# Two token halves as two runs of matmuls in w_out's and the feed-forward's units of a hybrid encoder step

## The chip, the cores and the metric

The kernel runs on one core of one Trainium2 chip. The metric is the device time of one execution in microseconds (us). TensorE multiplies, VectorE (DVE), ScalarE (ACT) and GpSimd (POOL) do the elementwise work, and SyncE (SP) issues the loads and stores.

## The reference

The program computes two layers of an encoder for 512 prompt tokens and 64 sample tokens. All of it is in f32.

```python
xn = rmsnorm(xp, norm_mix[l])
q, k, v, qi, ki, wi, u, gv = project(xn, w_in[l], pos_p)
a = dsa_prompt(q, qi, wi, k, v, ki, pos_p)
gvn = rmsnorm(jax.nn.gelu(gv), gate_norm[l])
bmix = jax.nn.gelu(u) * spatial_prompt(gvn, w_spatial[l], b_spatial[l])
xp = xp + jnp.concatenate([a, bmix], axis=-1) @ w_out[l]
xp = xp + sq_relu_ffn(rmsnorm(xp, norm_ffn[l]), w_ff1[l], w_ff2[l])

def sq_relu_ffn(x, w1, w2):
    h = jax.nn.relu(x @ w1)
    return (h * h) @ w2
```

The sample tokens go through the same lines with a cache of 128 positions. D_MODEL is 1024, D_FF is 4096. The change concerns the last two lines of a layer: the product with `w_out` and the two products of the feed-forward.

## The kernel before, in words

All 576 tokens (`TOK`) are kept side by side in the free dimension, with the model dimension on the partitions: `x`, `xh`, `xl`, `vh` and `vl` are 128 x 8 x 576, and the index of the 8 blocks of 128 (`KT`) is called k. A product in f32 precision is made of three matmuls on f32r numbers. Each f32 operand is split into a high part (`xh`, `vh`, `ring_hi`) and a low part (`xl`, `vl`, `ring_lo`), and the sum takes high by high, high weight by low activation, and low weight by high activation.

The weights stream from memory through a ring. SP loads 512 KB into `ring_raw`, ACT makes `ring_hi` from it (`split_hi`, line 521), DVE or POOL makes `ring_lo` (`split_lo`, line 766). There are four ring slots, and a slot is free when the unit that reads it is done (`unit_done`).

After the projection and the attention stage of a layer come 72 units (line 1309): 8 units of `w_out` (u = 0 to 7), then four groups of 8 units of `w_ff1` and 8 units of `w_ff2`. A unit makes 128 output features for all tokens. The 576 tokens are two halves of 288 (`HALVES`), because a PSUM bank holds 512 numbers, and unit u writes the banks 2 (u mod 4) and 2 (u mod 4) + 1. Per unit there are 8 k, three products and two halves: 48 matmuls of 128 x 288, and each carries its own weight load. Only the unit's last matmul raises `unit_done`, so nobody reads a bank ahead of the unit's end. In two layers this makes 144 units and 6912 matmuls.

TensorE's program is written out in order, with waits (`pe.wait_ge`) between the instructions. In the units these waits bear on the change:

- u = 0 (the first unit of `w_out`): its k run 4, 5, 6, 7, 0, 1, 2, 3, and ahead of k = 0 it waits for the last piece of `vl` (line 1325), which DVE makes in `mt_low` (line 928).
- u = 8, written `u == KT` (the first unit of `w_ff1`): ahead of each k it waits for `xl` of this k (line 1328). `xl` of block j is made by DVE in `feed` (line 772) from `x` and `xh` of block j, after ACT has made `xh` (line 536) and after DVE has added unit j's result to `x` (line 994). In DVE's program the order is: add unit j, `feed` of j - 1, `split_lo` of the next weights; and `feed` of block 7 stands behind the last `split_lo`.
- the first `w_ff2` unit of each group (`f == KT`): ahead of each k it waits for `vl` of this k (line 1331), which DVE makes at line 1017 from the results of the group's `w_ff1` unit k, after ACT's relu (line 730) and square (line 735).

Every other wait of a unit (`slot`, `unit_read`, line 1319) stands at its start.

Of the kernel before, what the change touches and what calls it, by code (L numbers as in the profile page):

```python
# [17 lines left out]
def hybrid_encoder_program(nc, A, O):  # L18
# [7 lines left out]
    SEQ, D = A["x_prompt"].shape[1], A["x_prompt"].shape[2]  # L26
    DEC = A["x_sample"].shape[1]
    DEPTH, _, PAST, NKV, HD = A["cache_k"].shape
    ID = A["cache_kidx"].shape[3]
    N_IN = A["w_in"].shape[2]  # L30
# [7 lines left out]
    KT = D // P  # L38
    FT = DFF // P
# [5 lines left out]
    NT = NPT + 1  # L45
# [45 lines left out]
    with ctx:  # L91
# [3 lines left out]
        def sem(name):  # L95
            return ctx.enter_context(nc.semaphore(name))
# [110 lines left out]
        xh_ready, vh_ready, vl_ready = sem("xh_ready"), sem("vh_ready"), sem("vl_ready")  # L207
# [12 lines left out]
        xl_ready = sem("xl_ready")  # L220
# [56 lines left out]
        def unit_read(u):  # L277

            l, u = u // UNITS, u % UNITS
            if u >= KT and (u - KT) % (2 * KT) < KT:  # L280
                f = (u - KT) // (2 * KT) * KT + (u - KT) % (2 * KT)
                return f1_relu, FT * l + f + 1
            j = u if u < KT else (u - KT) // (2 * KT) * KT + u % KT + KT
            return y_read, KT * (GROUPS + 1) * l + j + 1
# [776 lines left out]
        def _(pe):  # L1061
# [28 lines left out]
            for l in range(DEPTH):  # L1090
                def slot(n):

                    pe.wait_ge(lo_ready, SLOTS * l + n + 1)
                    return tuple(b[:, n % NSLOT, :] for b in (ring_hi, ring_lo))
# [60 lines left out]
                for n in range(S_OUT):  # L1155
                    w = slot(n)
# [152 lines left out]
                for u in range(UNITS):  # L1309
                    wh, wl = (b.rearrange("p (k n) -> p k n", k=KT) for b in slot(S_OUT + u))  # L1310
                    g, f = divmod(u - KT, 2 * KT)
                    first_product = u >= KT and f < KT
                    ah, al = (xh, xl) if first_product else (vh, vl)
                    if u >= 4:

                        pe.wait_ge(*unit_read(UNITS * l + u - 4))
                    if u == KT + 3:

                        pe.wait_ge(ssb_read, l + 1)

                    order = list(range(KT)) if u >= KT else list(range(KT // 2, KT)) + list(range(KT // 2))
                    for k in order:
                        if u == 0 and k == 0:

                            pe.wait_ge(vl_ready, (2 * NT + FT) * l + 2 * NT)
                        if u == KT:

                            pe.wait_ge(xl_ready, KT * (2 * l + 1) + k + 1)
                        if u >= KT and f == KT:

                            pe.wait_ge(vl_ready, (2 * NT + FT) * l + 2 * NT + KT * g + k + 1)
                        for w, a in ((wh, ah), (wh, al), (wl, ah)):
                            for half in range(2):
                                last = mm(bank[2 * (u % 4) + half][:, 0:HALF], w[:, k, :], a[:, k, HALVES[half]],  # L1334
                                          start=k == order[0] and w is wh and a is ah, stop=k == order[-1] and w is wl)
                    last.then_inc(unit_done, 1)
                    if u == KT + 1:

                        pe.wait_ge(ss_added, KT * (2 * l + 2))
                        for half in range(2):  # L1340
                            last = mm(bank[6 + half][:, 0:HALF], ones[:, :], ssacc[:, HALVES[half]], start=True, stop=True)
                        last.then_inc(ssb_done, 1)
# [53 lines left out]
```

## Time and profile before

| | |
|---|---|
| timed runs | 1470.62, 1472.02, 1513.19 us; median 1472.02 |
| the profiled execution: first to last instruction (span) | 1508.3 us, mean granted TensorE clock 0.919 |
| the profiled execution: time with what lies around the span | not given by itself; the slowest timed run, 1513.19 us, is 4.9 us above this span |
| TensorE matmul busy | 98% of the span, 9329 matmuls |
| TensorE weight load busy | 88%, 9329 loads |
| VectorE, ScalarE, GpSimd busy | 44%, 35%, 12% |

PE is TensorE's matmul row and PEld its weight-load row, which overlap. The end of a matmul is modelled, so the distance between the starts of two matmuls is what tells its real price. "PEclk" is the granted TensorE clock, as a share of 2.4 GHz: 1.0 is 2.4 GHz and 0.5 is 1.2 GHz. Times in the rows count from the first instruction.

### The profile page before, as it was taken

What the parts mean: (1) busy time and instruction counts of PE and PEld (TensorE: products, weight loads), DVE (VectorE), ACT (ScalarE), POOL (GpSimd) and SP (SyncE); (2) the same over time, 40 slices, a digit from 0 to 9 for tenths busy, and PEclk for the clock granted to TensorE, in tenths of its full rate; (3) what the DMA queues carried; (4) which work ended last, traced back from release to release, by engine and by line L of the source; (5) the groups of instructions that cost most, each with busy time, mean ns of one, the idle gap of its engine ahead of it and who ended that gap; (6) DMA issues with size and microseconds to landing.
All of it is one profiled execution on the core that took longest, in us unless ns stands there. A gap on an engine that the chain in (4) does not pass through costs nothing.

```text
span 1508.3 us, 22280 instructions
## 1 busy us (share of the span) xinstructions
PE 1483.1 (98%) x9329; PEld 1323.6 (88%) x9329; DVE 664.4 (44%) x1172; ACT 521.8 (35%) x956; POOL 185.1 (12%) x215
## 2 busy tenths in 40 slices
PE   6999999999999999999999999999999999999997
PEld 5766766899999999999976677669999999999997
DVE  5257632245444444444623683213454444344453
ACT  5365542233213223133335553323332231321322
POOL 4246200020000000000214540000100000000011
PEclk8999755799999999999999995559999999999998
DMA  6211200033232222222321120001322222222221
GB/s 180 70 57 43 74 5 0 0 85 85 85 84 78 82 80 85 84 84 83 104 82 45 40 78 25 5 1 42 85 75 82 83 84 84 85 85 85 82 59 63
DMA packets 169252, 102.37 MB, mean 68 GB/s; under 512 B 6920, under 2 KB 159424, under 8 KB 169152
## 3 DMA queue, kind: packets, MB, share of 16 engines
q1 hardware_dynamic: 169152, 100.94, 23.0%
q8 instruction: 74, 1.21, 0.3%
q14 instruction: 26, 0.21, 0.0%
HBM read 96.98 MB, written 3.95 MB: 67 GB/s over the span
## 4 chain that ended last, share of the span: by engine, by line
PE 97%; DVE 1%; DMA 1%; ACT 1%; issue 0%; SPq 0%; DVEq 0%; ACTq 0%
PE bank L1334 61%; PE bank L1108 15%; PE bank L1219 6%; PE bank L1255 4%; PE bank L1235 3%; PE bank L1126 2%; PE bank L1270 2%; PE bank L1286 1%; PE bank L1140 1%; DMA late<-in_x_prompt 1%; PE bank L1200 1%; PE bank L1353 0%; PE bank L1069 0%; PE bank L1085 0%; ACT L677 0%
## 5 line engine op out<-in xcount | busy, mean ns | idle before, releaser
L521 ACT ACTIVATE ring_hi<-ring_raw 128x1024 fp32r<-128x1024 f32 x176 | 184.8, 1050 | 305.4 <-PE bank L1334 248.6
L1334 PE MATMUL bank<-vh,ring_hi 128*128 128x288 f32 x1280 | 275.4, 296 | 0.0
L1334 PE MATMUL bank<-vl,ring_hi 128*128 128x288 f32 x1280 | 275.2, 296 | 0.0
L1334 PE MATMUL bank<-vh,ring_lo 128*128 128x288 f32 x1280 | 275.2, 296 | 0.0
L766 DVE TENSOR_TENSOR ring_lo<-ring_raw,ring_hi 128x1024 fp32r<-128x1024 f32 x164 | 213.6, 1302 | 132.5 <-ACT ring_hi L521 125.5
L1334 PE MATMUL bank<-xh,ring_hi 128*128 128x288 f32 x1024 | 220.8, 297 | 0.0
L1334 PE MATMUL bank<-xl,ring_hi 128*128 128x288 f32 x1024 | 220.2, 296 | 0.0
L1334 PE MATMUL bank<-xh,ring_lo 128*128 128x288 f32 x1024 | 220.2, 296 | 0.0
L1334 PEld LDWEIGHTS bank<-vh,ring_hi 128*128 128x128 f32 x1280 | 205.2, 189 | 0.0
L1334 PEld LDWEIGHTS bank<-vh,ring_lo 128*128 128x128 f32 x1280 | 205.2, 188 | 0.0
L1334 PEld LDWEIGHTS bank<-vl,ring_hi 128*128 128x128 f32 x1280 | 205.2, 189 | 0.0
L1334 PEld LDWEIGHTS bank<-xh,ring_hi 128*128 128x128 f32 x1024 | 164.3, 188 | 0.7 <-DVE xl L772 0.5
L1334 PEld LDWEIGHTS bank<-xh,ring_lo 128*128 128x128 f32 x1024 | 164.2, 188 | 0.0
L1334 PEld LDWEIGHTS bank<-xl,ring_hi 128*128 128x128 f32 x1024 | 164.2, 189 | 0.0
L1013 DVE TENSOR_TENSOR late<-late 128x576 f32<-128x576 f32 x64 | 48.6, 760 | 219.8 <-ACT late L730 219.8
L1025 DVE TENSOR_TENSOR late<-late,bank 128x288 f32<-128x288 f32 x128 | 52.4, 451 | 200.9 <-PE bank L1334 200.9
L730 ACT ACTIVATE late<-bank 128x288 f32<-128x288 f32 x128 | 45.7, 409 | 265.8 <-PE bank L1334 265.8
L1108 PE MATMUL bank<-ring_hi,xh 128*128 128x512 f32 (+1 forms) x320 | 133.7, 418 | 3.0 <-DVE xl L772 3.0
L1108 PE MATMUL bank<-ring_hi,xl 128*128 128x512 f32 (+1 forms) x320 | 126.9, 396 | 0.0
L1108 PE MATMUL bank<-ring_lo,xh 128*128 128x512 f32 (+1 forms) x320 | 126.8, 396 | 0.0
L406 POOL COPY ssacc<-late 128x576 f32<-128x576 f32 x5 | 3.5, 696 | 789.9 <-ACT late L540 789.9
L1219 PE MATMUL bank<-late 64*128 64x128 f32 (+4 forms) x160 | 100.2, 726 | 0.0
(161 smaller groups left out, 1608.9 us busy)
## 6 DMA issues: line engine op xcount, KB each, us to landing
ring_raw<-in_w_ff SPq DMA_DIRECT2D x128, 512.0 KB, 4.1
ring_raw<-in_w_in SPq DMA_DIRECT2D x32, 512.0 KB, 3.7
ring_raw<-in_w_out SPq DMA_DIRECT2D x16, 512.0 KB, 4.2
late<-in_x_prompt SPq DMA_DIRECT2D x4, 512.0 KB, 5.7
out_y_prompt<-late SPq DMA_DIRECT2D x4, 512.0 KB, 2.9
w_sp<-in_w_spatial SPq DMA_DIRECT2D x2, 512.0 KB, 4.2
gate_bc<-in_gate_norm SPq DMA_DIRECT2D x2, 256.0 KB, 4.9
out_k_prompt<-z SPq DMA_DIRECT2D x2, 256.0 KB, 4.3
```

The source lines that it names most:

```text
L521: s.activation(ring_hi[:, n % NSLOT, :], ring_raw[:, n % NRAW, :], ACT.Copy).then_inc(hi_ready, 1)
L730: last = s.activation(rl2[:, f % 2, HALVES[half]], bank[2 * (u % 4) + half][:, 0:HALF], ACT.Relu)
L766: v.tensor_tensor(ring_lo[:, n % NSLOT, :], ring_raw[:, n % NRAW, :], ring_hi[:, n % NSLOT, :].bitcast(F32), ALU.subtract).then_inc(lo_rea ...
L1013: link(v.tensor_tensor(h32[:, f % 2, :], rl2[:, f % 2, :], rl2[:, f % 2, :], ALU.mult))
L1025: last = v.tensor_tensor(yb[:, j % 2, HALVES[half]], r2b[:, HALVES[half]], bank[b + half][:, 0:HALF], ALU.mult)
L1108: last = mm(bank[t][0:ROWS[t], :], a[:, kx, cols(t)], b[:, kk, :], start=kx == 0 and b is wh and a is xh, stop=kx == KT - 1 and a is xl)
L1126: last = mm(bank[5 + i % 2][0:rows, 0:KEYS[t]], a[b:b + ID, hh // 4, cols(t)], k[b:b + ID, 0:KEYS[t]], start=a is qih and k is kh, stop=a ...
L1219: mm(bank[i % 2][0:ROWS[t], 0:KEYS[t]], qT[b:b + HD, hh % 4, cols(t)], keys[b:b + HD, 0:KEYS[t]], start=True, stop=True).then_inc(qk_done, 1)
L1235: last = tp(bank[2 + i % 2][0:n, c0:c0 + ROWS[t]], pr[0:ROWS[t], i % 2, s0:s0 + n], ident[0:ROWS[t], 0:ROWS[t]])
L1255: last = mm(bank[4 + a % 2][0:ROWS[t], hh * HD:(hh + 1) * HD], pT[0:n, i % 2, s * ROWS[t]:(s + 1) * ROWS[t]], vals, start=s == 0, stop=s = ...
L1270: last = mm(bank[6][0:rows, g * CPG:(g + 1) * CPG], w_spT[0:rows, g, 0:rows], gvn[0:rows, t, g * CPG:(g + 1) * CPG], start=True, stop=True)
L1334: last = mm(bank[2 * (u % 4) + half][:, 0:HALF], w[:, k, :], a[:, k, HALVES[half]], start=k == order[0] and w is wh and a is ah, stop=k == ...
```

## The change

The loop over the two halves moves from the innermost place of a unit to the outermost. Before, each weight tile was used for half 0 and then for half 1; now all 24 matmuls of half 0 (8 k by three products) come first, then all 24 of half 1. The waits inside the loop stay ahead of the first matmul of their k, which is now the one of half 0; half 1 waits for nothing. Lines behind the change are one higher than before (1335 for 1334).

```diff
-                    for k in order:
-                        if u == 0 and k == 0:
-
-                            pe.wait_ge(vl_ready, (2 * NT + FT) * l + 2 * NT)
-                        if u == KT:
-
-                            pe.wait_ge(xl_ready, KT * (2 * l + 1) + k + 1)
-                        if u >= KT and f == KT:
-
-                            pe.wait_ge(vl_ready, (2 * NT + FT) * l + 2 * NT + KT * g + k + 1)
-                        for w, a in ((wh, ah), (wh, al), (wl, ah)):
-                            for half in range(2):
+                    for half in range(2):
+                        for k in order:
+                            if half == 0:
+                                if u == 0 and k == 0:
+
+                                    pe.wait_ge(vl_ready, (2 * NT + FT) * l + 2 * NT)
+                                if u == KT:
+
+                                    pe.wait_ge(xl_ready, KT * (2 * l + 1) + k + 1)
+                                if u >= KT and f == KT:
+
+                                    pe.wait_ge(vl_ready, (2 * NT + FT) * l + 2 * NT + KT * g + k + 1)
+                            for w, a in ((wh, ah), (wh, al), (wl, ah)):
                                 last = mm(bank[2 * (u % 4) + half][:, 0:HALF], w[:, k, :], a[:, k, HALVES[half]],
                                           start=k == order[0] and w is wh and a is ah, stop=k == order[-1] and w is wl)
                     last.then_inc(unit_done, 1)
```

First place, on TensorE: the end of the first `w_ff1` unit (u = 8) of layer 0. In the kernel before, its last wait for `xl` (of k = 7) stands ahead of the 43rd of 48 matmuls, and the rows below are the last two matmuls of k = 6 and the six of k = 7:

```order
L1334 MATMUL bank0<-xh,ring_lo 128x288
L1334 MATMUL bank1<-xh,ring_lo 128x288
L1334 MATMUL bank0<-xh,ring_hi 128x288 [waits xl_ready]
L1334 MATMUL bank1<-xh,ring_hi 128x288
L1334 MATMUL bank0<-xl,ring_hi 128x288
L1334 MATMUL bank1<-xl,ring_hi 128x288
L1334 MATMUL bank0<-xh,ring_lo 128x288
L1334 MATMUL bank1<-xh,ring_lo 128x288
```

In the changed kernel the same wait stands ahead of the 22nd matmul, and half 1 (bank 1) begins behind it:

```order
L1335 MATMUL bank0<-xh,ring_lo 128x288
L1335 MATMUL bank0<-xh,ring_hi 128x288 [waits xl_ready]
L1335 MATMUL bank0<-xl,ring_hi 128x288
L1335 MATMUL bank0<-xh,ring_lo 128x288
L1335 MATMUL bank1<-xh,ring_hi 128x288
L1335 MATMUL bank1<-xl,ring_hi 128x288
L1335 MATMUL bank1<-xh,ring_lo 128x288
```

The wait has moved from 42 matmuls into the unit to 21; the number of matmuls and what each of them reads is the same.

Second place, on TensorE: the first `w_ff2` unit of the first group (u = 16), around its last wait for `vl` (k = 7). Before:

```order
L1334 MATMUL bank0<-vh,ring_lo 128x288
L1334 MATMUL bank1<-vh,ring_lo 128x288
L1334 MATMUL bank0<-vh,ring_hi 128x288 [waits vl_ready]
L1334 MATMUL bank1<-vh,ring_hi 128x288
L1334 MATMUL bank0<-vl,ring_hi 128x288
```

In the changed kernel:

```order
L1335 MATMUL bank0<-vh,ring_lo 128x288
L1335 MATMUL bank0<-vh,ring_hi 128x288 [waits vl_ready]
L1335 MATMUL bank0<-vl,ring_hi 128x288
L1335 MATMUL bank0<-vh,ring_lo 128x288
L1335 MATMUL bank1<-vh,ring_hi 128x288
```

Here too the last wait comes after 21 matmuls in place of 42. In the first unit of `w_out` the wait for the last `vl` comes after 12 matmuls in place of 24. On the other engines no instruction of the stage moves.

## Rows read from the trace of the kernel before

**Rows 1.** Page, parts 1 and 2: busy time by engine; granted clock in 40 slices.
```profile
PE 1483.1 (98%) x9329; PEld 1323.6 (88%) x9329; DVE 664.4 (44%) x1172; ACT 521.8 (35%) x956; POOL 185.1 (12%) x215
...
PEclk8999755799999999999999995559999999999998
```

**Rows 2.** Page, part 4: the chain that ended last, shares of the span by engine.
```profile
PE 97%; DVE 1%; DMA 1%; ACT 1%; issue 0%; SPq 0%; DVEq 0%; ACTq 0%
```

**Rows 3.** That chain in order of time: start us, us, what.
```profile
50.49 4.21 PE bank L1200 x32
...
356.39 396.81 PE bank L1334 x2976
```

**Rows 4.** w_ff1's first unit, layer 0: start us, us, line, count [idle before <-releaser].
```profile
342.04 0.32 PEld L1334 LDWEIGHTS bank<-xh,ring_hi 128*128 128x128 f32 x2
...
344.71 0.32 PEld L1334 LDWEIGHTS bank<-xl,ring_hi 128*128 128x128 f32 x2
...
347.95 0.30 PEld L1334 LDWEIGHTS bank<-xh,ring_hi 128*128 128x128 f32 x2 [0.25 <-DVE xl L772]
```

**Rows 5.** DVE in the same stretch.
```profile
342.37 0.82 DVE L994 TENSOR_TENSOR x<-x,bank 128x288 f32<-128x288 f32 x2 [1.60 <-PE bank L1334]
343.11 0.81 DVE L772 SCALAR_TENSOR_TENSOR xl<-x,gcol,xh 128x576 fp32r<-128x576 f32 x1
345.56 1.61 DVE L766 TENSOR_TENSOR ring_lo<-ring_raw,ring_hi 128x1024 fp32r<-128x1024 f32 x1 [1.64 <-ACT ring_hi L521]
347.09 0.80 DVE L772 SCALAR_TENSOR_TENSOR xl<-x,gcol,xh 128x576 fp32r<-128x576 f32 x1
```

**Rows 6.** Weight loads of the same unit in layer 1.
```profile
1079.49 0.32 PEld L1334 LDWEIGHTS bank<-xh,ring_hi 128*128 128x128 f32 x2
...
1085.39 0.30 PEld L1334 LDWEIGHTS bank<-xh,ring_hi 128*128 128x128 f32 x2 [0.25 <-DVE xl L772]
```

**Rows 7.** Weight loads of the first unit of w_ff2, layer 0, first group.
```profile
394.50 0.32 PEld L1334 LDWEIGHTS bank<-vh,ring_hi 128*128 128x128 f32 x2
...
397.17 0.32 PEld L1334 LDWEIGHTS bank<-vl,ring_hi 128*128 128x128 f32 x2
```

**Rows 8.** DVE in that stretch: the vl of k = 7.
```profile
396.37 0.76 DVE L1017 TENSOR_TENSOR vl<-late,vh 128x576 fp32r<-128x576 f32 x1
```

**Rows 9.** Weight loads at the start of w_out's first unit, layer 0.
```profile
290.47 0.42 PEld L1286 LDWEIGHTS bank<-ident,att 128*128 128x128 f32 x4 [1.61 <-DVE vl L928]
...
292.44 0.32 PEld L1334 LDWEIGHTS bank<-vh,ring_hi 128*128 128x128 f32 x2
```

**Rows 10.** DVE there: the last piece of vl.
```profile
291.80 0.69 DVE L928 TENSOR_TENSOR vl<-bank,vh 128x512 fp32r<-128x512 f32 x1 [1.44 <-ACT vh L702]
```

**Rows 11.** Page, part 5: one of six groups of the units' weight loads.
```profile
L1334 PEld LDWEIGHTS bank<-vh,ring_hi 128*128 128x128 f32 x1280 | 205.2, 189 | 0.0
```

**Rows 12.** Matmuls of the projection's start, in time; six in a row share a bank.
```profile
19.52 0.77 PE L1108 MATMUL bank<-ring_hi,xh 128*128 128x512 f32 x1 [3.02 <-DVE xl L772]
20.09 0.63 PE L1108 MATMUL bank<-ring_lo,xh 128*128 128x512 f32 x1
...
22.22 0.62 PE L1108 MATMUL bank<-ring_hi,xh 128*128 128x512 f32 x1
...
23.37 0.40 PE L1108 MATMUL bank<-ring_lo,xh 128*128 128x512 f32 x1
23.61 0.40 PE L1108 MATMUL bank<-ring_hi,xl 128*128 128x512 f32 x1
23.84 0.40 PE L1108 MATMUL bank<-ring_hi,xh 128*128 128x512 f32 x1
```

**Rows 13.** Three stretches: busy us by engine, then granted clock, DMA share, GB/s.
```profile
19.50:22.70 3.20, 3.18 (x8) 2.52 (x9) 2.11 (x2) 3.20 (x6) 1.98 (x3) 0.50 0.00 0
...
289.00:292.50 3.50, 2.00 (x17) 2.03 (x17) 2.02 (x4) 0.60 (x1) 0.00 (x0) 1.00 0.02 5
1494.00:1500.50 6.50, 5.65 (x27) 5.66 (x28) 1.90 (x4) 1.86 (x4) 1.28 (x5) 0.50 0.01 3
```

## The prediction, made before the changed kernel was run

> **What bounds the kernel now.** I read the busy shares first: PE is busy for 98% of the span and no other engine for half of it [rows 1]. A busy PE may still be a waiting one, so next comes the chain of waits: PE holds 97% of it [rows 2]. In order of time the units of w_out and of the feed-forward are one unbroken run: 2976 matmuls in 396.81 us, which is 133.3 ns from one start to the next [rows 3]. So a unit of 48 matmuls lasts 6.40 us, half a unit 3.20 us, and the 6912 matmuls 922 us, more than half of the time. The granted clock is full there; it is low in the attention stage and at the ends [rows 1]. Whatever changes the 133.3 ns, or makes PE wait in the units, changes the time by the same amount. Whatever makes another engine faster or slower does not, as long as its result arrives before PE asks for it.
>
> The reader should also see that PE already waits in one place: in the first unit of w_ff1 the weight load for k = 7 stands with an idle time put down to DVE's xl, in layer 0 at 347.95 and in layer 1 at 1085.39 [rows 4, 6]. A wait that is already late in the old order is what the new order moves ahead.
>
> **The change part by part.** It removes and adds no matmul, no weight load, no semaphore and no DMA. It moves two things: which matmul follows which, and how early in a unit the waits for xl and vl stand. The unit still reports its end with its last matmul, so DVE and ACT get nothing sooner.
>
> *The distance of two matmuls.* Before, neighbours write alternate banks; now 24 in a row accumulate into one bank. The units of before don't show this, but two other places do. In the projection six matmuls in a row share a bank, with the same pattern of operands (a stationary tile used twice, then a new one): the starts 23.37 and 23.61 lie inside such a run, and 23.61 to 23.84 crosses to the next bank; both distances are 0.23 to 0.24 us [rows 12]. At line 1200 the small projection runs 16 matmuls of 288 columns into one bank and then 16 into another: 4.21 us for 32, 131.6 ns each [rows 3]. Its stationary tiles are narrower (80 and 40 columns), which may account for the 1.7 ns to 133.3. The bounds are therefore -1.7 ns by line 1200, and above, by the projection: its 512 columns take 0.232 us at full clock, and (22.22 - 20.09)/5 = 0.426 us at clock 0.5 [rows 12, 13], so streaming alone would be 0.213 us at full clock, and 19 ns come on top. For 288 columns streaming is 0.120 us, and 13 ns come on top now. If the difference of 6 ns were the price of staying in a bank, it would be +6 ns. I take 0, the value of the bank crossing, which tests just this: 6912 x 0 = 0, with ends of -12 and +41 us.
>
> *The first unit of w_ff1 (u = 8), once a layer.* Its first weight load starts at 342.04 [rows 4]. In the new order k = 7 comes after 21 matmuls, at 342.04 + 21 x 0.1333 = 344.84; in the old one after 42, at 347.64, where it really came at 347.95. What sets the 347.95 is DVE's second xl, which runs from 347.09 for 0.80 us and ends at 347.89 [rows 5], so PE resumes 0.06 us behind it. Does this xl come sooner in the new kernel? DVE's program has it behind a split of the weights (345.56 for 1.61 us), which itself waits for ACT's half of that split, and the chain starts with the addition at 342.37, when unit 7 is done [rows 5]. None of these looks at unit 8, so they stay where they are. PE then waits from 344.84 until 347.95: 3.11 us, where the old wait cost 0.31. The difference is 2.80 us, which is just the 21 matmuls that the old order still had to do ahead of it. k = 6 needs the first xl, which ends at 343.92 and is asked for at 344.44: no wait. Layer 1 is the same: 1079.49 + 2.80 = 1082.29 against 1085.39 now, 3.10 us of waiting, and 1085.39 less 1085.09 before [rows 6]. Sum: 2 x 2.80 = +5.6 us. Nothing gives it back later: behind the wait stand only PE's own matmuls, all other engines wait for PE, and the tail of the kernel comes after them.
>
> *The first unit of w_ff2 in each group, eight times.* k = 7 is now asked for at 394.50 + 21 x 0.1333 = 397.30, the second load of the row at 397.17 [rows 7]. Its vl ends at 396.37 + 0.76 = 397.13 [rows 8]; with the 0.06 us of above PE could go at 397.19, so 0.11 us are left. All eight groups have this distance within 0.01 us in the trace. I take 0. Cover gone, a late vl costs what the late xl costs now, 0.3 us: at most 8 x 0.3 = 2.4 us.
>
> *The first unit of w_out, once a layer.* k = 0 is asked for after 12 matmuls, at 292.44, the thirteenth load [rows 9]; the last vl ends at 291.80 + 0.69 = 292.49, so PE goes at 292.55 [rows 10]: +0.1 us, two layers +0.2 us.
>
> The sum is 0 + 5.6 + 0 + 0.2 = +5.8 us. On the profiled execution that makes a span of 1508.3 + 5.8 = 1514.1 us. That execution lies 36 us above the median of the runs, beside the slowest of them; the waits above are made of DVE and ACT times at places where PE's clock is full, so I carry the same 5.8 us to the median: 1472.0 + 5.8 = 1477.8 us.
>
> **The rivals.**
>
> *A. PE's clock falls in the new wait.* In this trace the clock is at 0.5 from 19.5 us, right behind 3.02 us in which PE waited, and again in the tail at 1494 to 1500.5 [rows 12, 13]. Against it: ahead of w_out's first unit PE's weight loads stand idle for 1.61 us, and the clock stays at 1.0 through it [rows 9, 13]. The new wait is 3.1 us, twice that. If the clock fell for as long as in the tail, 6.5 us, matmuls would start every 133.3 x 0.426/0.232 = 245 ns and 6.5 x (1 - 133.3/245) = 3.0 us would be lost, twice: 1477.8 + 6.0 = 1483.8 us. The Trainium skill, "TensorE: Matmul & The Clock Gate", section "Why this matters for your kernels", says that an idle gap between bursts of matmuls sends the engine back to half rate; by that rule this rival is the case, and the trace so far agrees with it at 19.5 us and does not at the 1.61 us gap.
>
> *B. Staying in one bank costs time (the slow side).* 6 ns a matmul, worked out above, from the first unit on and in every one: 1477.8 + 41 = 1519 us. For it speaks only that the projection, which stays in a bank for six, has the larger remainder over streaming. Against it speak line 1200's 131.6 ns and the bank crossing that is no faster.
>
> *C. New stationary tiles cost, kept ones don't.* In the old order four of six matmuls have the tile of their predecessor, in the new one two of six. If all of the 13 ns over streaming (80 ns in six) came from the two switches, each would cost 40 ns, and four cost 160: +80 ns x 1152 sixes = +92 us, 1570 us. Against it: each matmul carries its own load, of 189 ns, more than the 133.3 ns between matmuls, so loads overlap whether the tile is new or not [rows 11]; and between 342.04 and 344.71 ten pairs of loads start 0.267 us apart, the same from hi to hi and from hi to lo [rows 4]. The Trainium skill, same page, section "Step-by-step: what each phase is for", says that loading is kept apart from multiplying so that one can "load once and matmul repeatedly", and by this the new order is the worse one; the trace shows no reuse for either order to lose.
>
> *D. A run in one bank is quicker,* as line 1200: -12 us, 1477.8 - 12 = 1466 us. Its narrower tiles explain that as well.
>
> That the change does not do what it says is excluded by the order of the instructions: the waits do stand at the 22nd matmul.
>
> **How the numbers follow.** My forecast of 1477.8 us gets 0.73, A 0.13, B 0.05, C 0.03, D 0.06. The range takes in the forecast, D at 1466, and A at 1483.8 with the 2.4 us of the eight vl: 1466 to 1487 us. It leaves out B and C. About 2%, 29 us, is what a measurement of this kernel can tell from no change. Forecast, A and D lie within it; B and C are slower: 0.08. D with a larger size than line 1200 shows is all that could be faster: 0.02. The rest, 0.90, is within 2%.
>
> **What would show it.** Right: the weight load of k = 7 in unit 8 starts 2.8 us late of its free place in both layers, with an idle time of about 3 us put down to xl; the long run of the units still has 133.3 ns a matmul; the eight vl waits are absent or under 0.1 us. Rival A would show a granted clock under 1.0 behind 348 us; B, C and D another distance in every unit. The forecast is wrong if xl of k = 7 ends sooner than 5.8 us after unit 8 begins, or if the distance moves by more than a nanosecond.

## The result, and the profile after

The changed kernel takes 1522.91 us (median of 4 runs, 1518.21 to 1527.72). The kernel before, now with four runs, has 1470.62, 1472.02, 1511.31 and 1513.19 us. The ratio is 1.0351 with a 95% interval of 1.0289 to 1.0412, so by this ratio the change is slower by more than 2%. The forecast was 1477.8 us with a range of 1466 to 1487: wrong, and far off.

The kernel before has two levels, a rare one near 1472 us and a common one near 1512 us, and the ratio compares with its two runs on the rare level; against the two others the change is 0.7%, some 10 us. Both parts need a cause: the 10 us, and the 40 us between the levels.

The page of the changed kernel, parts 1 and 2, beside [rows 1]:

```profile
span 1525.7 us, 22280 instructions
...
PE 1495.5 (98%) x9329; PEld 1333.6 (87%) x9329; DVE 664.8 (44%) x1172; ACT 521.8 (34%) x956; POOL 185.1 (12%) x215
...
PEclk8999755699999999999999995559999999999999
```

The other engines work as long as before, within 0.4 us. The clock row has the same two valleys, slices 5 to 8 and 25 to 27, which are the attention stages of the two layers.

The chain in order of time (start us, us, what), beside [rows 3]:

```profile
298.24 51.30 PE bank L1335 x384
...
355.12 13.03 PE bank L1335 x75
...
369.11 396.79 PE bank L1335 x2976
```

The long run of the units is unchanged: 396.79/2976 = 133.3 ns. What is new stands between 298.24 and 369.11. In the kernel before, the same stretch, from the first unit of w_out to the long run at 356.39 [rows 3], reads:

```profile
291.13 56.80 PE bank L1334 x426
347.95 7.47 PE bank L1334 x54
```

And in layer 1 of the changed kernel:

```profile
1040.16 52.74 PE bank L1335 x384
...
1098.48 11.77 PE bank L1335 x75
1111.22 396.81 PE bank L1335 x2976
```

The stretch has grown from 356.39 - 291.13 = 65.26 us to 70.87 us in layer 0 and to 71.06 us in layer 1. The weight loads of unit 8 in layer 0, beside [rows 4], are the first, the last ahead of k = 7, and three behind the wait:

```profile
349.23 0.19 PEld L1335 LDWEIGHTS bank<-xh,ring_hi 128*128 128x128 f32 x1
...
351.90 0.19 PEld L1335 LDWEIGHTS bank<-xh,ring_lo 128*128 128x128 f32 x1
355.11 0.29 PEld L1335 LDWEIGHTS bank<-xh,ring_hi 128*128 128x128 f32 x1 [3.03 <-DVE xl L772]
355.28 0.33 PEld L1335 LDWEIGHTS bank<-xl,ring_hi 128*128 128x128 f32 x1
355.52 0.33 PEld L1335 LDWEIGHTS bank<-xh,ring_lo 128*128 128x128 f32 x1
```

k = 7 was free to start at 349.23 + 2.80 = 352.03 and started at 355.11: 3.08 us. DVE, beside [rows 5], shows why; xl ends at 354.25 + 0.81 = 355.06:

```profile
352.75 1.58 DVE L766 TENSOR_TENSOR ring_lo<-ring_raw,ring_hi 128x1024 fp32r<-128x1024 f32 x1 [1.65 <-ACT ring_hi L521]
354.25 0.81 DVE L772 SCALAR_TENSOR_TENSOR xl<-x,gcol,xh 128x576 fp32r<-128x576 f32 x1
```

Layer 1, beside [rows 6]:

```profile
1098.48 0.19 PEld L1335 LDWEIGHTS bank<-xh,ring_hi 128*128 128x128 f32 x1 [3.04 <-DVE xl L772]
```

Behind the wait the loads are 0.24 us apart in place of 0.133. Five stretches of the changed kernel (busy us of PE, PEld, DVE, ACT, POOL with their counts, then the granted clock) say why: unit 7 ahead of the wait, 24 matmuls behind it, the next unit, the place behind the wait of layer 1, and the start of layer 1's w_out.

```profile
343.00:349.00 6.00, 6.00 (x47) 6.00 (x47) 3.15 (x4) 2.31 (x3) 1.43 (x1) 1.00 0.31 84
...
355.20:361.00 5.80, 5.80 (x24) 5.80 (x25) 0.00 (x0) 0.00 (x0) 0.00 (x0) 0.50 0.32 90
362.00:368.00 6.00, 6.00 (x48) 6.00 (x47) 2.74 (x3) 2.13 (x4) 0.00 (x0) 1.00 0.15 41
...
1098.70:1101.80 3.10, 3.10 (x14) 3.10 (x14) 0.00 (x0) 0.00 (x0) 0.00 (x0) 0.50 0.61 169
1040.60:1043.90 3.30, 3.30 (x16) 3.30 (x15) 0.69 (x1) 0.19 (x1) 0.00 (x0) 0.50 0.00 0
```

The clock is at 0.5 behind the wait, in both layers; PE is "busy" in each of these stretches, but does about half as many matmuls per microsecond. At 1040.60 it is at 0.5 behind the short wait ahead of w_out too, which is as long as before. This loss of some 1.5 us is not the change's: in a second profile of the kernel before (before_again, below) layer 0 has it as well, and its 426 matmuls take 58.32 us in place of 56.80.

```profile
298.07 58.32 PE bank L1334 x426
```

```profile
298.40:301.60 3.20, 3.20 (x16) 3.20 (x15) 0.69 (x1) 0.30 (x1) 0.00 (x0) 0.51 0.02 5
```

Last, the two other places. The first unit of w_ff2 reaches k = 7 at 410.02, and its vl ends at 409.08 + 0.76 = 409.84: no wait (beside [rows 7, 8]). The first unit of w_out is due at 299.55 and loads at 299.65 (beside [rows 9]):

```profile
409.88 0.19 PEld L1335 LDWEIGHTS bank<-vh,ring_lo 128*128 128x128 f32 x1
410.02 0.19 PEld L1335 LDWEIGHTS bank<-vh,ring_hi 128*128 128x128 f32 x1
```

```profile
409.08 0.76 DVE L1017 TENSOR_TENSOR vl<-late,vh 128x576 fp32r<-128x576 f32 x1
```

```profile
299.42 0.19 PEld L1335 LDWEIGHTS bank<-vh,ring_lo 128*128 128x128 f32 x1
299.65 0.19 PEld L1335 LDWEIGHTS bank<-vh,ring_hi 128*128 128x128 f32 x1
```

A trap in the groups of part 5, before and after:

```profile
L1334 PE MATMUL bank<-vh,ring_lo 128*128 128x288 f32 x1280 | 275.2, 296 | 0.0
```

```profile
L1335 PE MATMUL bank<-vh,ring_lo 128*128 128x288 f32 x1280 | 379.3, 296 | 0.0
```

The busy time of this group rose from 275.2 to 379.3 us, at the same count and the same mean. Nothing got longer: a group's overlapping instructions are counted once, and in the old order its two matmuls stood next to each other. The distance between starts is what has to be compared.

### The profile page after: what moved, and what is told of

It is laid out like the page before. It is cut to its first block, busy times and chain, and to the rows that moved or that the text cites. A ratio compares the mean times of both kernels' runs of the same rounds, so it can differ in the third digit from the quotient of the medians.

```text
span 1525.7 us, 22280 instructions
## 1 busy us (share of the span) xinstructions
PE 1495.5 (98%) x9329; PEld 1333.6 (87%) x9329; DVE 664.8 (44%) x1172; ACT 521.8 (34%) x956; POOL 185.1 (12%) x215
## 4 chain that ended last, share of the span: by engine, by line
PE 97%; DVE 1%; ACT 1%; DMA 1%; issue 0%; SPq 0%; DVEq 0%; ACTq 0%
PE bank L1335 60%; PE bank L1108 15%; PE bank L1219 6%; PE bank L1255 4%; PE bank L1235 3%; PE bank L1126 2%; PE bank L1270 2%; PE bank L1286 1%; PE bank L1140 1%; DMA late<-in_x_prompt 1%; PE bank L1200 1%; PE bank L1354 0%; PE bank L1069 0%; DVE ring_lo L766 0%; DVE xl L772 0%
## 5 line engine op out<-in xcount | busy, mean ns | idle before, releaser
L1335 PE MATMUL bank<-vh,ring_lo 128*128 128x288 f32 x1280 | 379.3, 296 | 0.0
L1335 PE MATMUL bank<-vl,ring_hi 128*128 128x288 f32 x1280 | 379.1, 296 | 0.0
L1335 PE MATMUL bank<-vh,ring_hi 128*128 128x288 f32 x1280 | 378.9, 296 | 0.0
L1335 PE MATMUL bank<-xh,ring_hi 128*128 128x288 f32 x1024 | 305.1, 298 | 5.6 <-DVE xl L772 5.6
L1335 PE MATMUL bank<-xl,ring_hi 128*128 128x288 f32 x1024 | 304.7, 298 | 0.0
L1335 PE MATMUL bank<-xh,ring_lo 128*128 128x288 f32 x1024 | 304.6, 297 | 0.0
L1335 PEld LDWEIGHTS bank<-vl,ring_hi 128*128 128x128 f32 x1280 | 241.1, 188 | 0.0
L1335 PEld LDWEIGHTS bank<-vh,ring_hi 128*128 128x128 f32 x1280 | 241.0, 188 | 0.0
L1335 PEld LDWEIGHTS bank<-vh,ring_lo 128*128 128x128 f32 x1280 | 240.8, 188 | 0.0
L1335 PEld LDWEIGHTS bank<-xl,ring_hi 128*128 128x128 f32 x1024 | 194.3, 190 | 0.1
```

## The experiments

Two theories were on the table. W: the change costs its waits (5.8 us) and the clock behind them, and the 40 us are the attention stage's clock, which falls out differently from run to run. Q: the new order itself costs time in all units, or holds the attention stage at the low clock.

**before_again and after_again.** No edit; the two kernels, timed again.

> The kernel before, unchanged, to see which times it takes and with which granted clock. Theory W (waits): the change costs 5.8 us of waits and some 6 us of lower clock behind them, and all that lies beyond is the clock of the attention stage, which differs from run to run by chance. Theory Q: the new order itself holds the attention stage at the lower clock in every run. Both expect here runs near 1471 us and runs near 1512 us, as in the four runs so far, the slower ones with the lower mean clock and nothing in between.

> The changed kernel, unchanged. W: every run lies about 12 us above one of the two levels of before, so near 1483 or near 1524 us, and some of the runs are at 1483. Q: all runs at 1515 us or more, none within 15 us of 1483.

before_again: 1510.0 to 1518.6 us in six runs, median 1517.38, none on the rare level; the eleven runs of before taken beside it have one at 1477.79 us with clock 0.947, and ten at 1506.6 to 1518.3 with clocks of 0.914 to 0.925, mean 1512.8. after_again: 1515.4 to 1528.6 us, median 1521.56, mean 1521.6. So the rare level is rare: in all runs of this study the kernel before was on it 4 times in 39. The change is 8 us above the common level. W's 12 us were too much, and its runs near 1483 us did not appear here. Q is not excluded by these two. The two sets of the unchanged kernel differ by 3 us in the means of their common level (1515.8 and 1512.8 us), so sets of this size tell the price of the change to some 3 us only. The profile of after_again has the clock at 0.5 behind the wait in both layers: the 75 matmuls there would take 10.0 us at 133.3 ns.

```profile
356.16 11.53 PE bank L1335 x75
...
1093.47 11.52 PE bank L1335 x75
```

**unit8_old.** Two runs per unit everywhere but in the first unit of w_ff1.

```diff
-                    for half in range(2):
-                        for k in order:
+                    if u != KT:
+                        ...
+                    else:
+                        for k in order:
+                            ...
+                                for half in range(2):
```

> The new order in all units but the first one of w_ff1 in each layer, which keeps the alternating halves. W: the wait of 3.1 us and the fall of the clock behind it are gone, and the runs lie on the levels of before, 1471 and 1512 us, within 1 us. Q: the runs of matmuls are still there in 142 of 144 units, so all runs are above 1505 us.

Measured 1512.48 to 1517.53 us in five runs and 1472.41 in one; median 1513.19. Both levels of before are back, though 142 of 144 units still have the new order: Q falls, in both of its forms. (The five runs spread over 5 us, where W had said 1 us; so do the runs of before.)

**unit8_new_only.** The opposite: the new order in that unit alone (`if u == KT:`).

> The old alternating order in all units but the first one of w_ff1 in each layer, which alone has its two halves as two runs. Theory W (the price is the wait there, 5.6 us, and the fall of the clock behind it): the whole difference between the changed kernel (mean 1522 us in ten runs) and the common level of before (1514 us) is here again, 1522 us within 3 us, with a wait of 3.1 us in each layer and a clock of 0.5 behind it. Theory Q (142 other units in runs cost something too): at most half of it, under 1518 us.

Four runs at 1517.3 to 1526.6 (mean 1521.1, with before at 1511.1 beside them in eleven runs) and two at 1483.4 and 1489.0. Two units of 144 carry the whole price, +10 us here against 8 to 9 us for the changed kernel, and its runs on the lower level lie 11 to 17 us above the 1472 of before; W had 12. That level was within reach of a kernel with the wait, so the wait does not abolish it. In its profile the clock stays up behind the wait of layer 0 and is down behind that of layer 1, against W's 0.5 in both: 27 matmuls at 133.3 ns are 3.6 us.

```profile
350.50 3.85 PE bank L1336 x27
...
1090.69 5.14 PE bank L1336 x27
```

**feed_first.** The new order everywhere, and DVE makes the last block of xl ahead of the last split of the weights.

```diff
+                    if j == KT - 1:
+                        feed(KT - 1, KT * (2 * l + 1), 2 * l + 1)
                     split_lo(N0 + S_OUT + j + NSLOT)
-                feed(KT - 1, KT * (2 * l + 1), 2 * l + 1)
```

> The new order everywhere, and in DVE's program the last block of xl is made ahead of the last split of the weights in place of behind it. W: that xl ends some 3 us sooner, at about the time at which PE asks for it; the wait shrinks from 3.1 us to 0.1 us and the clock does not fall, so 1471 and 1512 us again, within 1 us. Q: all runs above 1505 us.

Median 1512.82 us (1509.75 to 1518.38), before's common level. DVE's rows in layer 0 show the two blocks of xl side by side, ending at 352.02, ahead of the split:

```profile
350.27 1.75 DVE L772 SCALAR_TENSOR_TENSOR xl<-x,gcol,xh 128x576 fp32r<-128x576 f32 x2
352.72 1.67 DVE L766 TENSOR_TENSOR ring_lo<-ring_raw,ring_hi 128x1024 fp32r<-128x1024 f32 x1 [0.70 <-ACT ring_hi L521]
```

In its chain, layer 1's first ten units are one run again: 480 matmuls in 64.12 us, 133.6 ns each.

```profile
1029.82 64.12 PE bank L1336 x480
1094.91 396.81 PE bank L1336 x2976
```

So the 8 to 10 us come from the late xl, and nothing else in the new order costs more than the 3 us that these sets can tell; warm_first, below, is finer.

**warm_l0 and warm_both.** They test the 40 us. In the attention stage PE is busy all the time by the profile and yet at half clock most of the time. The stage of layer 0 (three stretches, with a short one at the full clock between two at half) and that of layer 1, in the kernel before:

```profile
173.00:200.00 27.00, 27.00 (x93) 19.77 (x93) 7.25 (x28) 9.08 (x33) 2.53 (x2) 0.50 0.13 35
200.20:206.80 6.60, 6.60 (x49) 4.28 (x48) 4.14 (x17) 5.04 (x24) 0.00 (x0) 1.00 0.02 4
207.10:285.40 78.30, 78.30 (x275) 53.63 (x274) 17.88 (x50) 22.93 (x65) 3.80 (x3) 0.50 0.01 2
903.40:1022.70 119.30, 119.30 (x424) 82.28 (x424) 30.07 (x95) 38.16 (x124) 6.33 (x5) 0.50 0.04 12
```

Its work is narrow: scores with 64 of 128 rows, products with 64 columns, transposes. The edit, on the kernel before, adds products over the whole array, whose result is overwritten. They stand ahead of each of the 40 items of a stage (a tile of tokens and a head): two where it has fewer than 384 keys (the short rows) and three where it has 384 or more (in warm_l0 only where `l == 0`):

```diff
+                    if i == 0:
+                        pe.wait_ge(hi_ready, SLOTS * l + S_OUT + 1)
+                    warm = ring_hi[:, S_OUT % NSLOT, :]
+                    for _ in range(2 if KEYS[t] < 3 * P else 3):
+                        mm(bank[i % 2][:, 0:CW], warm[:, 0:P], warm[:, 0:CW], start=True, stop=True)
                     b = HD * (hh // 4)
```

> The kernel before, with idle multiplications added to the attention stage of layer 0 alone: ahead of each of 40 score products two (three for the long rows) 128x512 products of weights that nobody reads, into the bank that the scores then overwrite. Theory C (the rare runs near 1472 us are runs in which one of the two attention stages keeps its clock): layer 0's attention stays at clock 1.0, takes some 75 to 85 us in place of 117, and every run lies between 1470 and 1490 us. Rival (the rare level has another cause): the added 96 products cost their 20 to 40 us, the time is 1530 to 1555 us and the clock of the stage 0.5 as before.

> The same products added in both layers. C: both attention stages at clock 1.0, and every run between 1430 and 1460 us, below all runs of before. Rival: 1550 to 1590 us.

warm_l0: 1486.18 us (1482.48 to 1491.37), ratio 0.9838, interval 0.9811 to 0.9865. warm_both: 1463.93 us (1463.25 to 1467.71), ratio 0.9694, interval 0.9675 to 0.9713, 4 us above the range that C had set. C missed in warm_l0 too, by less: layer 0's stage takes some 98 us in place of 75 to 85, and one run of the four lies 1.4 us above the range. The two attention stages of warm_l0, with and without the added products:

```profile
172.00:270.00 98.00, 96.37 (x555) 64.13 (x554) 32.88 (x104) 41.50 (x133) 6.36 (x5) 1.00 0.05 14
882.30:998.30 116.00, 116.00 (x430) 80.79 (x429) 30.67 (x98) 39.41 (x128) 6.32 (x5) 0.53 0.04 12
```

More work takes less time, because it is done at the full clock. The rival, by which the products would only cost, falls. What in the stage's own work keeps the clock low is not shown: it differs from the added products in its rows and columns, in its transposes and in its operands (plain f32, where the added ones are f32r), and no run separates these. The kernel is 1511.92 - 1486.18 = 26 us shorter with 96 products in it, which at 0.232 us each [rows 12] are 22 us; as an estimate, without them a stage at full clock would be up to 48 us shorter than at half clock. The two levels are 40 us apart, so less than one stage is enough to make them. In warm_both the valleys of the clock row are gone:

```profile
PEclk9999999999999999999999999999999999999999
```

**warm_thin.** One added product for the short rows and two for the long ones, in both layers.

> In both layers one product for the short rows and two for the long ones, 56 a layer in place of 96. C: if that is enough for the clock, some 8 us a layer less than with 96, 1415 to 1445 us; if it is not, the clock falls in part of the stages and the runs scatter between 1440 and 1530 us. Rival: 1535 to 1560 us.

One run at 1453.76 us with clock 0.989 and three at 1530.7 to 1533.1 with 0.930. The same program has two levels, 78 us apart; the profiled one lost the clock in the middle of the stage:

```profile
172.00:199.00 27.00, 27.00 (x156) 18.12 (x156) 11.79 (x44) 14.36 (x57) 2.54 (x2) 1.00 0.16 45
199.60:298.40 98.80, 98.80 (x318) 63.13 (x318) 17.91 (x51) 23.05 (x66) 3.81 (x3) 0.50 0.01 2
```

**warm_both_again, warm_after, warm_first.** With the attention stage held at the full clock the runs lie within a few us, and the change can be measured by itself: warm_after is the changed kernel with the added products, warm_first is feed_first with them.

> The kernel before with the added products in the attention stage of both layers, unchanged from the run above, as the measure for the next three. Every theory expects 1464 us within 3 us, and a clock of 0.99.

> The changed kernel (two runs per unit in all units) with the same added products. With the attention stage out of the way, W expects the two waits of 2.80 us more than before and 0.1 us twice, 5.8 us, and 1.5 to 3.0 us in each layer for the clock behind the wait: 1464 + 9 to 12 = 1473 to 1476 us. The forecast's likeliest case without a fall of the clock would be 1470 us. Q: 1480 us or more.

> The changed kernel, the added products, and the last block of xl made ahead of the last split. W: no wait but 0.1 us at four places, no fall of the clock behind it, and the same distance of matmuls: 1464 us within 2 us, the same as the old order. Q (runs of one bank cost something in the 6912 matmuls): 1467 us or more.

Medians 1463.28 (1461.85 to 1463.87), 1471.03 (1468.47 to 1473.10) and 1461.34 us (1460.71 to 1463.32). All runs of warm_after lie above all runs of the other two: the change costs 7.75 us, and with xl made in time it costs nothing. warm_after came out 2 us under what W had set. Its profile says why: behind the wait of layer 0 the clock is 0.50, and behind the same wait in layer 1 it is 1.00, with 24 matmuls where the other has 14.

```profile
327.20:330.40 3.20, 3.20 (x14) 3.20 (x15) 0.00 (x0) 0.00 (x0) 0.00 (x0) 0.50 0.57 169
1041.90:1045.00 3.10, 3.10 (x24) 3.10 (x25) 0.00 (x0) 0.00 (x0) 0.00 (x0) 1.00 0.61 169
```

**warm_first_22.** Two added products everywhere.

> As the run above, with two added products for the long rows too, 80 a layer in place of 96. If two are enough for the clock, 32 x 0.23 = 7 us less, 1457 us; if not, the clock falls in the attention stage of the last two tiles and the time is 1470 to 1500 us.

Median 1454.14 us (1451.44 to 1455.42), below all 39 runs of the kernel before. It is the best version found, and the new order is in it; what it gains comes from the clock and not from the order.

## Why the prediction was wrong, step by step

- *The distance of two matmuls, taken as 0:* right. 133.3 ns before and after; warm_first is 2 us under warm_both_again. Rivals B, C and D did not occur. That a neighbouring piece of code crosses from one bank to the next at the same distance was the right row to trust.
- *The first unit of w_ff1, +2.80 us a layer:* right. 3.08 us in layer 0 against a forecast of 3.11, with an idle time put down to xl, at the place named. feed_first shows that DVE's order is the cause.
- *The first units of w_ff2, 0, and of w_out, +0.1 us:* right, 0 and 0.1.
- *The clock keeps through the new wait:* wrong. This was rival A, which got 0.13. In the four profiles with this wait (after, after_again, unit8_new_only, warm_after) the clock is at 0.5 behind it in six of eight places. Both rows that A was judged by misled. The clock that stayed at 1.0 through the wait of 1.61 us [rows 9, 13] was one outcome of two: behind the same wait ahead of w_out it is at 0.5 in 8 of the 28 places of all profiles (two layers in each of 14), before_again among them. And the clock at 0.5 at 19.5 us [rows 13] had not fallen in the 3.02 us of waiting ahead of it: it was low before that wait began, so this row spoke neither for A nor against it.

```profile
12.40:16.00 3.60, 2.51 (x14) 2.18 (x15) 0.00 (x0) 1.31 (x3) 0.00 (x0) 0.51 1.11 230
```

The Trainium skill ("TensorE: Matmul & The Clock Gate", section "Why this matters for your kernels") says that an idle gap between bursts of matmuls sends the engine back to half rate; six of the eight places agree with it, two do not. A's price of 3.0 us a layer was too high in five of the six: 11 to 14 matmuls start 0.24 us apart in place of 0.133, and with the first distance behind the wait this loses 1.4 to 1.6 us; in layer 0 of the first profile it is 25 matmuls and 2.9 us. With a fall of 1.5 us in six of eight places the likeliest sum would have been 5.8 + 2 x 0.75 x 1.5 = 8 us, and 7.75 was measured.
- *"I carry the same 5.8 us to the median":* wrong, and this step alone put the result out of the range: 1472 + 8 = 1480 us lies within it. The median of the three runs was the rare level, with two of three runs on it by chance; the profiled execution, 36 us above it, was the common one. The text noted that distance and did not ask where it came from, although the clock row shows 0.5 through both attention stages. 1513.2 us, the run beside the profile, plus 8 us would have been 1521.
- *"About 2% is what a measurement can tell":* the levels are 40 us, 2.7%, apart, so with few runs a change of nothing can look like 2.7% either way. The forecast had no case in which the base moves.

Open: no run on the rare level was profiled. That the clock of an attention stage makes the 40 us is argued from the mean clock of such runs (0.947 to 0.949 against 0.914 to 0.925) and from the price of a stage in warm_l0, and not seen. That the whole of one stage keeps its clock there does not fit well. An estimate: a run spends 2 x (1 - mean clock) of its span at half clock, which is 150 and 156 us for the two rare runs of before whose clock is on record, and 242 us in the mean (226 to 261) for its common ones. Some 90 us are gone, and a whole stage has 105 to 123 us at half clock. The longer low stretch of layer 0's stage, of 78.3 us, would at the full clock be 39 us shorter, which is the distance of the two levels; so a rare run may be one in which the clock stays up from the short stretch at 200.20 on. What decides between the levels in a given run is not known. That the changed kernel itself was on the common level in all ten of its runs may be chance: at 4 of 39 for before it would happen one time in three.

## What to carry to other kernels

When a loop is turned so that an operand's last part is asked for earlier, count how many instructions stand ahead of each wait before and after, and compare with the row that ends the wait: here the wait could be forecast to a tenth of a microsecond, and the clock behind it could not. The remedy is then often in the order of the engine that makes the operand, as with feed_first. And before a difference is carried to a median, ask whether the profiled execution belongs to the same level as the median; a granted clock of 0.5 through a stage in which TensorE is always busy means that full-array work added there may pay.

## What was not expected of the hardware

- TensorE, 100% busy by the profile, stayed at 1.2 GHz for 78 to 122 us with f32 matmuls of 64 rows or 64 columns and transposes. Adding 96 full-array products a layer brought it to 2.4 GHz and shortened the kernel by 48 us, from 1511.92 to 1463.93.
- The same program falls on two levels: 1472 and 1512 us for the kernel before, 1454 and 1532 us for warm_thin.
- Behind the same wait of 3.1 us the clock was at 0.5 in six of eight places and at 1.0 in two; behind the same wait of 1.6 us ahead of w_out it was at 0.5 in 8 of 28.
